# Differential attention normalised from PSUM, and weight chunks split in pieces of 1024 and 512 columns

## The chip, the core and the metric

The kernel runs on one core of a Trainium2 chip. TensorE (PE in the profile) multiplies matrices and writes them to PSUM; VectorE (DVE), ScalarE (ACT) and GpSimd (POOL) work element by element; SyncE (SP) issues most DMAs. GpSimd touches SBUF only. The metric is the device time of one execution in microseconds (us).

## The reference

Two blocks run one after the other on 512 tokens of width 1024, all in float32. The first has a dilated attention layer and a grouped state-space layer. The second has four layers: differential attention, a gated recurrence (hgrn2), a sliding-window attention with sinks, and differential attention again; each is followed by a feed-forward part (1024 to 4096 and back) and a gate. What the change touches most is the differential attention, which occurs twice:

```python
def diff_attention(h, w_in, lam, subln, w_out, rel_bias, layer_idx):
    ...
    lam_full = jnp.exp(jnp.sum(lam32[0] * lam32[1])) - jnp.exp(jnp.sum(lam32[2] * lam32[3])) + lam_init
    for blk in range(S // BLOCK):
        qs = blk * BLOCK
        ke = qs + BLOCK
        s = jnp.einsum('bmqd,bmkd->bmqk', q[:, :, qs:ke], k[:, :, :ke]).astype(jnp.float32)
        ...
        s = jnp.where(rel >= 0, s + bias, -jnp.inf)
        a = jax.nn.softmax(s, axis=-1).reshape(B, H, 2, BLOCK, ke)
        a = a[:, :, 0] - lam_full * a[:, :, 1]
        outs.append(jnp.einsum('bhqk,bhkv->bhqv', a.astype(v.dtype), v[:, :, :ke]))
    ...
```

Eight heads each have two maps of scores (m = 0 and 1). Each is softmaxed by itself, and the second, scaled by lambda, is taken from the first.

## The kernel before, in words

All weights come as one stream of 270 chunks of 128 x 2048 float32 (1 MB). SyncE loads a chunk into one of two raw buffers, raw[0] and raw[1]. GpSimd splits it: the cast (L311) writes the high part wh in the reduced format fp32r, and the subtraction (L313) writes the low part wl = raw - wh. Each large product is then three matmuls (L351 to L353): high by high, low by high, high by low. There are two buffers of wh and wl. GpSimd begins to split chunk c when TensorE has used up chunk c-2 (semaphore w_used); TensorE begins chunk c when w_split says that its subtraction has ended. The very first chunk is split by lines of its own (L318, L323).

The differential attention (function diff_attention) goes in four runs r of two heads each. A run has eight jobs n: head hh = n // 4, block of 128 queries b = n % 4, so a job's scores are w = 128, 256, 384 or 512 columns wide. For a job:

- TensorE computes two maps of scores (L1414) into the PSUM banks 2 + 2 * (n % 2) + m.
- VectorE adds the bias (L1568, L1569) and writes the sum to the SBUF tile SC, then takes the negated row maxima of both maps (L1573).
- ScalarE takes the exponential of both (L1488), in place in SC, with the row sums into sa columns 4 and 5, by an accumulator that a second instruction reads out.
- VectorE normalises in four instructions: the reciprocal of the sums (L1580); times lambda, one column (L1581); the second map times that column (L1582); and the first map times its reciprocal plus the second map (L1583).
- TensorE transposes the result (L1423), ScalarE copies it from PSUM (L1496, tile PT), TensorE multiplies it by V (L1438), and ScalarE copies that out (L1501).

The order on TensorE is written out by hand in pe_jobs: scores(0), scores(1), a piece of the next run's projection; then for each job j: transposes(j), scores(j + 2), a piece of projection (fill), values(j). A run projects for the next run three chunks in eight pieces, the first four of 24 matmuls with 512 columns, the last four of 24 matmuls with 256. In the last run nothing is left to project, and six of the eight finished heads are transposed in its place (turn_head). On VectorE, dve_jobs puts biased(j) behind normalise(j - 1). On ScalarE, act_jobs puts the exponentials of job j ahead of the copy of job j - 1 and the copying out of job j - 2.

Semaphores of a job: SC_FREE after the bias has been added, BIASED after the maxima, EXPED after the exponentials, PNORM after the normalisation, PTC after the copy of the transposes, PV after the product by V. GpSimd has in the differential attention the splits and a few small steps on the heads' norms (L1375, L1376).

Of the kernel before, what the change touches and what calls it, by code (L numbers as in the profile page):

```python
# [14 lines left out]
F32 = mybir.dt.float32  # L15
F32R = mybir.dt.float32r
I32 = mybir.dt.int32
ALU = mybir.AluOpType
ACT = mybir.ActivationFunctionType
# [9 lines left out]
CHUNK = 2048  # L29
# [198 lines left out]
def build(nc, t, out):  # L228

    ctx = ExitStack()  # L230
    with ctx:
# [21 lines left out]
        raw = [sb(f"raw{i}", [P, CHUNK]) for i in range(RAW)]  # L253
        wh = [sb(f"wh{i}", [P, CHUNK], F32R) for i in range(SPLIT)]
# [46 lines left out]
        def load_chunk(sp, c, slot):  # L301

            sp.wait_ge(w_split.h, c - RAW + 1)
            sp.dma_start(raw[slot][:, :], t["weights"][bass.ds(c, 1)].rearrange("a p n -> p (a n)")).then_inc(raw_in[slot].h, 16)

        def split_chunk(pool, c, r, s):

            pool.wait_ge(w_used.h, CREDIT + c - SPLIT + 1)
            pool.wait_ge(raw_in[r].h, 16 * ((c - r) // RAW + 1) if isinstance(c, int) else (c - r) * (16 // RAW) + 16)
            pool.sem_inc(split_ready.h, 1)  # L310
            pool.tensor_copy(wh[s][:, :], raw[r][:, :]).then_inc(w_high.h, 1)  # L311
            pool.wait_ge(w_high.h, c + 1)
            pool.tensor_tensor(wl[s][:, :], raw[r][:, :], wh[s][:, :].bitcast(F32), ALU.subtract).then_inc(w_split.h, 1)  # L313

        def split_high(pool, k):

# [1018 lines left out]
        def diff_attention(layer, j):  # L1335
            c0 = pos[0]
            lam_init = 0.8 - 0.6 * math.exp(-0.3 * layer)
            with ExitStack() as c:
# [20 lines left out]
                with nc.Block() as block:  # L1359
# [26 lines left out]
                    def _(pe):  # L1386
# [19 lines left out]
                        def run(r):  # L1406
                            def wait(s, k):
                                pe.wait_ge(s.h, s.base + RUN * r + k)

                            def scores(n):  # L1410
                                hh, b = n // 4, n % 4
                                wait(SC_FREE, n - 1)
                                for m in range(2):
                                    x = nc.tensor.matmul(PS[2 + 2 * (n % 2) + m][:, 0:P * (b + 1)],  # L1414
                                                         QT[64 * m:64 * m + 64, r % 2, hh, P * b:P * b + P],
                                                         KTT[64 * m:64 * m + 64, r % 2, hh, 0:P * (b + 1)], start=True, stop=True)
                                x.then_inc(SC_DONE.h, 1)

                            def transposes(n):
                                wait(PNORM, n + 1)  # L1420
                                wait(PTC, n)
                                for k in range(n % 4 + 1):
                                    x = nc.tensor.transpose(PS[TBANK][:, P * k:P * k + P], SC[:, n % 2, 0, P * k:P * k + P], ident[:, :])  # L1423
                                x.then_inc(TR.h, 1)

                            def fill(j):
                                for n in range(RUN):
                                    if STEP[n] == j and r + 1 < RUNS:
                                        project(r + 1, n)
                                if r + 1 == RUNS and 0 <= j < 6:  # L1430
                                    turn_head(j)

                            def values(n):
                                wait(PTC, n + 1)
                                wait(OEV, n)
                                hh, b = n // 4, n % 4
                                for k in range(b + 1):
                                    x = nc.tensor.matmul(PS[OBANK][:, 0:P], PT[:, n % 2, P * k:P * k + P],  # L1438
                                                         V[:, r % 2, k, P * hh:P * hh + P], start=(k == 0), stop=(k == b))
                                x.then_inc(PV.h, 1)  # L1440
                            wait(PEV, RUN)
                            pe_jobs(RUN, 2, scores, transposes, values, fill)
# [8 lines left out]
                    def _(act):  # L1451
# [28 lines left out]
                        def run(r):  # L1480
# [3 lines left out]
                            def exps(n):  # L1484
                                wait(BIASED, n + 1)
                                w = P * (n % 4 + 1)
                                for m in range(2):
                                    x = a.activation(SC[:, n % 2, m, 0:w], SC[:, n % 2, m, 0:w], ACT.Exp,  # L1488
                                                     bias=sa[:, n % 2, 2 + m:3 + m], accum_out=sa[:, n % 2, 4 + m:5 + m])
                                x.then_inc(EXPED.h, 1)  # L1490

# [49 lines left out]
                    def _(dve):  # L1541
# [15 lines left out]
                        def run(r):  # L1557
                            def wait(s, k):
                                dve.wait_ge(s.h, s.base + RUN * r + k)

                            def biased(n):
                                hh, b = n // 4, n % 4
                                w = P * (b + 1)
                                wait(SC_DONE, n + 1)
                                wait(TR, n - 1)
                                if n == 0:
                                    dve.wait_ge(BIAS_IN.h, BIAS_IN.base + 16 * (r + 1))
                                link(v.tensor_tensor(SC[:, n % 2, 0, 0:w], PS[2 + 2 * (n % 2)][:, 0:w], B[:, 2 * hh, WD - w:WD], ALU.add))  # L1568
                                v.tensor_tensor(SC[:, n % 2, 1, 0:w], PS[3 + 2 * (n % 2)][:, 0:w], B[:, 2 * hh + 1, WD - w:WD], ALU.add).then_inc(SC_FREE.h, 1)  # L1569
                                wait(SC_FREE, n + 1)  # L1570
                                if n == 7:
                                    dve.sem_inc(BIAS_USED.h, 1)
                                v.tensor_reduce(sa[:, n % 2, 2:4], SC[:, n % 2, :, 0:w], AX.X, ALU.max, negate=True).then_inc(BIASED.h, 1)  # L1573
                                if r + 1 == RUNS and 2 <= n < 8:
                                    low_head(n - 2)

                            def normalise(n):
                                w = P * (n % 4 + 1)
                                wait(EXPED, n + 1)
                                link(v.reciprocal(sa[:, n % 2, 6:8], sa[:, n % 2, 4:6]))  # L1580
                                link(v.tensor_tensor(sa[:, n % 2, 7:8], sa[:, n % 2, 7:8], lam[:, 261:262], ALU.mult))  # L1581
                                link(v.tensor_scalar(SC[:, n % 2, 1, 0:w], SC[:, n % 2, 1, 0:w], sa[:, n % 2, 7:8], None, ALU.mult))  # L1582
                                v.scalar_tensor_tensor(SC[:, n % 2, 0, 0:w], SC[:, n % 2, 0, 0:w], sa[:, n % 2, 6:7],  # L1583
                                                       SC[:, n % 2, 1, 0:w], ALU.mult, ALU.add).then_inc(PNORM.h, 1)
                            dve_jobs(RUN, 2, biased, normalise)
                        for r in range(RUNS):
# [1867 lines left out]
```

## Time and profile before

| | us |
|---|---|
| median of 3 runs | 3903.22 |
| lowest and highest | 3902.64, 3917.36 |
| the profiled execution, own time | 3908.86 |
| its span from first to last instruction | 3907.1 |
| PE busy | 3601.4 |
| DVE busy | 1652.6 |
| ACT busy | 910.5 |
| POOL busy | 1902.8 |

The profile lists the instructions of that one execution. A row of a group gives line, engine, operation, output and input tiles, shapes and count, then the busy time and the mean duration of one. A row of waits says which instruction stood ready behind whose work, how long in all, how many times, and the longest. The granted clock is the share of full speed at which TensorE was let run: 1.0 is 2.4 GHz and 0.5 is 1.2 GHz, and a mean over a stretch lies between. The parts of the program, in us from the start of the span: the dilated attention to 670, the state-space layer to 1040, the first differential attention 1040 to 1290 (its runs 0 to 2 from 1072 to 1237), then feed-forward, hgrn2 from 1760, feed-forward, sliding-window attention from 2570, feed-forward, the second differential attention 3180 to 3440 (its runs 0 to 2 from 3213 to 3385), and the last feed-forward.

### The profile page before, as it was taken

The page shows a single profiled execution, that of the slowest core. Times are in us where ns is not written, and L with a number is a line of the kernel's source. Part 1 is how long each engine was busy: PE and PEld are TensorE (multiplying, and loading weights), DVE is VectorE, ACT ScalarE, POOL GpSimd, SP SyncE. Part 2 cuts the span into 40 slices and gives each one's busy share as a digit, 9 for nine tenths or more (in the row PEclk, how much of TensorE's full clock was granted, in tenths as well). Part 3 has the DMA queues.
Part 4 walks back from the last instruction along what each step waited for, and adds up shares of the span by engine and source line. Part 5 has one row for each costly group of instructions (what it writes and reads, how often), then busy time and mean ns, then how long its engine had stood idle before and what let it go on. Part 6 is the DMA issues. An engine that isn't in the chain of part 4 may idle for free. (4 is left out here: it accounts for less than half of the span.)

```text
span 3907.1 us, 49897 instructions
## 1 busy us (share of the span) xinstructions
PE 3601.4 (92%) x19658; PEld 2934.7 (75%) x19658; DVE 1652.6 (42%) x2665; ACT 910.5 (23%) x2424; POOL 1902.8 (49%) x733
## 2 busy tenths in 40 slices
PE   8899997799998899999957999998999998889999
PEld 6787874677775788878756888776888877678887
DVE  5522326898366411144375211355311326641114
ACT  2333333223134111011251111134101123411101
POOL 5444440523532455555644555532565553245554
PEclk9999995888998999999978999999999999899999
DMA  4236881244221222222202222221222221122222
GB/s 135 92 110 102 109 119 55 68 111 106 104 76 55 90 100 97 97 86 89 86 2 81 87 97 97 87 98 60 87 97 97 97 95 69 55 92 97 97 97 76
DMA packets 96732, 346.76 MB, mean 89 GB/s; under 512 B 27414, under 2 KB 46230, under 8 KB 61720
## 3 DMA queue, kind: packets, MB, share of 16 engines
q1 hardware_dynamic: 84176, 318.31, 27.4%
q10 hardware_dynamic: 12360, 25.70, 1.9%
q8 instruction: 140, 2.29, 0.2%
q14 instruction: 56, 0.46, 0.0%
HBM read 320.90 MB, written 18.87 MB: 87 GB/s over the span
## 5 line engine op out<-in xcount | busy, mean ns | idle before, releaser
L311 POOL CAST wh<-raw 128x2048 fp32r<-128x2048 f32 x269 | 515.7, 1917 | 1623.1 <-PE bank L353 1310.5
L313 POOL TENSOR_TENSOR wl<-raw,wh 128x2048 fp32r<-128x2048 f32 x269 | 1247.1, 4636 | 21.5
L351 PE MATMUL bank<-XTh,wh 128*128 128x512 f32 (+1 forms) x2448 | 951.0, 388 | 32.4 <-DVE XTl L1200 15.1
L352 PE MATMUL bank<-XTh,wl 128*128 128x512 f32 (+1 forms) x2448 | 935.7, 382 | 0.0
L353 PE MATMUL bank<-XTl,wh 128*128 128x512 f32 (+1 forms) x2448 | 935.4, 382 | 0.0
L351 PEld LDWEIGHTS bank<-XTh,wh 128*128 128x128 f32 x2448 | 467.5, 191 | 143.1 <-issue 30.5
L353 PEld LDWEIGHTS bank<-XTl,wh 128*128 128x128 f32 x2448 | 466.4, 191 | 89.8
L352 PEld LDWEIGHTS bank<-XTh,wl 128*128 128x128 f32 x2448 | 467.7, 191 | 84.6
L352 PE MATMUL bank<-wh,HTl 128*128 128x512 f32 x1024 | 403.4, 394 | 0.0
L351 PE MATMUL bank<-wh,HTh 128*128 128x512 f32 x1024 | 401.7, 392 | 0.0
L353 PE MATMUL bank<-wl,HTh 128*128 128x512 f32 x1024 | 397.4, 388 | 0.0
L351 PE MATMUL bank<-wh,XTh 128*128 128x512 f32 (+2 forms) x992 | 367.4, 370 | 29.2 <-DVE XTl L1200 12.6
L353 PE MATMUL bank<-wl,XTh 128*128 128x512 f32 (+2 forms) x992 | 360.7, 364 | 0.0
L352 PE MATMUL bank<-wh,XTl 128*128 128x512 f32 (+2 forms) x992 | 360.6, 364 | 0.0
L1119 ACT ACTIVATE R<-bank 128x512 f32<-128x512 f32 x128 | 76.6, 598 | 946.6 <-PE bank L353 946.6
L1218 DVE TENSOR_TENSOR bank<-R,bank 128x512 f32<-128x512 f32 x128 | 89.1, 696 | 428.8 <-ACT R L1119 428.8
L351 PEld LDWEIGHTS bank<-wh,XTh 128*128 128x128 f32 x992 | 191.7, 193 | 71.2 <-issue 28.1
L351 PEld LDWEIGHTS bank<-wh,HTh 128*128 128x128 f32 x1024 | 192.2, 188 | 44.7
L353 PEld LDWEIGHTS bank<-wl,HTh 128*128 128x128 f32 x1024 | 192.2, 188 | 43.0
L1697 DVE TENSOR_TENSOR SC<-bank,B 128x512 f32<-128x512 f32 (+2 forms) x128 | 59.5, 517 | 382.7 <-PE bank L1653 382.3
L352 PEld LDWEIGHTS bank<-wh,HTl 128*128 128x128 f32 x1024 | 192.5, 188 | 38.1
L353 PEld LDWEIGHTS bank<-wl,XTh 128*128 128x128 f32 x992 | 191.4, 193 | 28.9
(375 smaller groups left out, 4143.0 us busy)
## 6 DMA issues: line engine op xcount, KB each, us to landing
raw<-in_weights SPq DMA_DIRECT2D x270, 1024.0 KB, 4.8
B<-bias_d ACTq DMA_DIRECT2D x8, 1024.0 KB, 5.6
B<-bias_a ACTq DMA_DIRECT2D x8, 512.0 KB, 13.4
bias_d<-O SPq DMA_DIRECT2D x16, 256.0 KB, 21.9
MO<-HS SPq DMA_DIRECT2D x64, 64.0 KB, 2.6
bc<-in_ln_g ACTq DMA_DIRECT2D x8, 512.0 KB, 6.8
bc<-in_ln_b ACTq DMA_DIRECT2D x8, 512.0 KB, 7.7
X<-in_x SPq DMA_DIRECT2D x4, 512.0 KB, 7.9
```

The lines of the kernel that those rows point to most:

```text
L311: pool.tensor_copy(wh[s][:, :], raw[r][:, :]).then_inc(w_high.h, 1)
L313: pool.tensor_tensor(wl[s][:, :], raw[r][:, :], wh[s][:, :].bitcast(F32), ALU.subtract).then_inc(w_split.h, 1)
L351: nc.tensor.matmul(psum, sh, mh, start=first, stop=False)
L352: nc.tensor.matmul(psum, sl, mh, start=False, stop=False)
L353: return nc.tensor.matmul(psum, sh, ml, start=False, stop=last)
L1119: nc.scalar.activation(R[u % 2][:, :], up_bank(q, u)[:, :], ACT.Relu).then_inc(rest["relu"].h, 1)
L1218: v.tensor_tensor(b, R[u % 2][:, :], b, ALU.mult).then_inc(rest["square"].h, 1)
L1697: r = v.tensor_tensor(o, s, b.unsqueeze(1).to_broadcast([P, m, w]), ALU.add)
```

## The change

It has two edits. The first lets ScalarE write the exponentials to the two PSUM banks that held the job's scores, instead of to SC. VectorE then reads them there: the product by 1/sum and the product by lambda are one instruction with two scalar columns, which writes SC, and the last instruction takes its first map from PSUM. The scores of job n, which overwrite the banks of job n - 2, wait for the normalisation (PNORM) of job n - 2 where they waited for its SC_FREE. The second edit divides each chunk's cast into two instructions of 1024 columns and its subtraction into four of 512. The semaphores are raised by the last piece, so nobody downstream gets a part of a chunk earlier.

```diff
+        def pieces(n):
+            return [slice(CHUNK // n * i, CHUNK // n * (i + 1)) for i in range(n)]
+
         def split_chunk(pool, c, r, s):
...
             pool.sem_inc(split_ready.h, 1)
-            pool.tensor_copy(wh[s][:, :], raw[r][:, :]).then_inc(w_high.h, 1)
+            for half in pieces(2):
+                x = pool.tensor_copy(wh[s][:, half], raw[r][:, half])
+            x.then_inc(w_high.h, 1)
             pool.wait_ge(w_high.h, c + 1)
-            pool.tensor_tensor(wl[s][:, :], raw[r][:, :], wh[s][:, :].bitcast(F32), ALU.subtract).then_inc(w_split.h, 1)
+            for quarter in pieces(4):
+                x = pool.tensor_tensor(wl[s][:, quarter], raw[r][:, quarter], wh[s][:, quarter].bitcast(F32), ALU.subtract)
+            x.then_inc(w_split.h, 1)
...
                             def scores(n):
                                 hh, b = n // 4, n % 4
-                                wait(SC_FREE, n - 1)
+                                wait(PNORM, n - 1)
...
                                 for m in range(2):
-                                    x = a.activation(SC[:, n % 2, m, 0:w], SC[:, n % 2, m, 0:w], ACT.Exp,
+                                    x = a.activation(PS[2 + 2 * (n % 2) + m][:, 0:w], SC[:, n % 2, m, 0:w], ACT.Exp,
                                                      bias=sa[:, n % 2, 2 + m:3 + m], accum_out=sa[:, n % 2, 4 + m:5 + m])
...
                                 link(v.reciprocal(sa[:, n % 2, 6:8], sa[:, n % 2, 4:6]))
-                                link(v.tensor_tensor(sa[:, n % 2, 7:8], sa[:, n % 2, 7:8], lam[:, 261:262], ALU.mult))
-                                link(v.tensor_scalar(SC[:, n % 2, 1, 0:w], SC[:, n % 2, 1, 0:w], sa[:, n % 2, 7:8], None, ALU.mult))
-                                v.scalar_tensor_tensor(SC[:, n % 2, 0, 0:w], SC[:, n % 2, 0, 0:w], sa[:, n % 2, 6:7],
+                                link(v.tensor_scalar(SC[:, n % 2, 1, 0:w], PS[3 + 2 * (n % 2)][:, 0:w], sa[:, n % 2, 7:8], lam[:, 261:262],
+                                                     ALU.mult, ALU.mult))
+                                v.scalar_tensor_tensor(SC[:, n % 2, 0, 0:w], PS[2 + 2 * (n % 2)][:, 0:w], sa[:, n % 2, 6:7],
                                                        SC[:, n % 2, 1, 0:w], ALU.mult, ALU.add).then_inc(PNORM.h, 1)
```

## Rows read from the trace of the kernel before

**Rows 1.** The page's first part: busy us (share of span) x instructions of each engine

```profile
PE 3601.4 (92%) x19658; PEld 2934.7 (75%) x19658; DVE 1652.6 (42%) x2665; ACT 910.5 (23%) x2424; POOL 1902.8 (49%) x733
```

**Rows 2.** Waits of PE, 1072 to 1237, then 3213 to 3380: us, times, longest

```profile
PE bank L1423 <- DVE SC L1583: 10.4, 9, 4.2
PE bank L1438 <- ACT PT L1496: 4.4, 5, 1.2
...
PE bank L1423 <- DVE SC L1583: 15.9, 8, 5.7
```

**Rows 3.** Timeline from 1181.9 (start, us, instruction, [idle before])

```profile
1181.94 2.01 DVE L1582 TENSOR_SCALAR SC<-SC,sa 128x128 f32<-128x128 f32 x1
...
1183.94 4.50 POOL L313 TENSOR_TENSOR wl<-raw,wh 128x2048 fp32r<-128x2048 f32 x1
1183.98 4.61 DVE L1583 SCALAR_TENSOR_TENSOR SC<-SC,sa 128x128 f32<-128x128 f32 x1
...
1188.65 0.47 PE L1423 MATMUL bank<-ident,SC 128*128 128x128 f32 x1 [4.22 <-DVE SC L1583]
```

**Rows 4.** Single lines of the attention: duration ns min/median/max, first and last start, forms

```profile
L1582 DVE TENSOR_SCALAR SC<-SC,sa x64: 286/420/4807, 1079.2 to 3422.5; 128x128 f32<-128x128 f32 x16, 128x256 f32<-128x256 f32 x16, 128x384 f32<-128x384 f32 x16, 128x512 f32<-128x512 f32 x16
...
L1583 DVE SCALAR_TENSOR_TENSOR SC<-SC,sa x64: 350/617/4612, 1079.5 to 3423.1; 128x128 f32<-128x128 f32 x16, 128x256 f32<-128x256 f32 x16, 128x384 f32<-128x384 f32 x16, 128x512 f32<-128x512 f32 x16
...
L1581 DVE TENSOR_TENSOR sa<-sa,lam x64: 158/159/3554, 1075.6 to 3422.3; 128x1 f32<-128x1 f32 x64
```

**Rows 5.** Single lines outside it, the same columns

```profile
L1218 DVE TENSOR_TENSOR bank<-R,bank x128: 695/696/697, 1354.7 to 3796.8; 128x512 f32<-128x512 f32 x128
...
L1189 DVE SCALAR_TENSOR_TENSOR bank<-bank,st,bc x64: 747/759/760, 1322.8 to 3850.5; 128x512 f32<-128x512 f32 x64
```

**Rows 6.** Groups by shape, DVE, 1239 to 1277 (last run, no chunk): busy us, mean ns

```profile
L1583 DVE SCALAR_TENSOR_TENSOR SC<-SC,sa 128x512 f32<-128x512 f32 x2 | 1.5, 750 | 0.1
...
L1582 DVE TENSOR_SCALAR SC<-SC,sa 128x512 f32<-128x512 f32 x2 | 1.0, 486 | 0.1
```

**Rows 7.** Stretches: us, busy us (instructions) of each engine, granted clock, DMA share, GB/s

```profile
1190.00:1200.00 10.00, 10.00 (x37) 6.89 (x33) 3.24 (x8) 2.67 (x9) 1.25 (x1) 0.74 0.24 96
...
1072.00:1237.00 165.00, 149.52 (x850) 119.74 (x849) 108.32 (x168) 59.17 (x214) 61.75 (x20) 0.97 0.22 75
3213.00:3385.00 172.00, 152.02 (x848) 122.21 (x848) 113.91 (x168) 59.16 (x214) 61.23 (x20) 0.94 0.21 70
...
670.00:1040.00 370.00, 327.21 (x1993) 267.68 (x1994) 290.92 (x373) 92.11 (x180) 156.24 (x74) 0.89 0.37 105
```

**Rows 8.** The sigmoid on ScalarE: duration ns min/median/max

```profile
L1126 ACT ACTIVATE Y<-bank x16: 598/598/604, 1710.5 to 3869.2; 128x512 f32<-128x512 f32 x16
L1126 ACT ACTIVATE bank<-bank x16: 582/582/582, 1744.2 to 3902.0; 128x512 f32<-128x512 f32 x16
```

**Rows 9.** GpSimd: a one-column instruction, a chunk under the feed-forward, who waited for L313

```profile
L958 POOL TENSOR_SCALAR st<-st x32: 191/192/193, 1322.9 to 3850.2; 128x1 f32<-128x1 f32 x32
...
1506.57 1.90 POOL L311 CAST wh<-raw 128x2048 fp32r<-128x2048 f32 x1 [4.45 <-PE bank L353]
1508.55 4.63 POOL L313 TENSOR_TENSOR wl<-raw,wh 128x2048 fp32r<-128x2048 f32 x1
...
  PE bank L351: 5.3, 5
```

**Rows 10.** Timelines of the norm at 728, the sinks, the first attention

```profile
728.09 4.33 DVE L831 SCALAR_TENSOR_TENSOR N<-X,st,bc 128x1024 f32<-128x1024 f32 x1
...
732.48 1.97 PE L754 MATMUL bank<-ident,N 128*128 128x128 f32 x8 [3.49 <-DVE N L831]
...
2597.95 4.07 DVE L1709 TENSOR_SCALAR stats<-stats,sk 128x2 f32<-128x2 f32 x1
...
117.73 4.81 DVE L1721 TENSOR_TENSOR SC<-SC,stats 128x512 f32<-128x512 f32 x1
```

**Rows 11.** Timeline of DVE in the state-space layer

```profile
752.42 4.87 DVE L2859 TENSOR_TENSOR W<-scratch 128x512 f32<-128x512 f32 x1
```

## The prediction

> **What bounds the kernel now.** The page's first part comes first: TensorE is busy 92% of the span, VectorE 42%, GpSimd 49% [rows 1]. The So time comes back only where TensorE stands still, or runs at half clock after standing still. PE was not busy for 306 us in all (3907.1 less 3601.4), and the change touches one place directly: the two differential attentions, some 250 us each. Each has four runs of eight jobs. In runs 0 to 2 TensorE also projects the next run's queries, keys and values, and GpSimd splits their weight chunks beside it; the fourth run has no projection and no chunk.
>
> The waits of PE in runs 0 to 2 name one releaser above all: the transposes (L1423) waited 10.4 and 15.9 us for VectorE's last step of the normalisation (L1583) [rows 2]. The timeline tells why. At 1181.94 the normalisation's second product (L1582, 128x128) took 2.01 us, and its third (L1583) took 4.61 us; GpSimd's subtraction had started at 1183.94 and took 4.50. PE stood still for 4.22 us [rows 3]. The quickest L1582 took 286 ns and the quickest L1583 350 ns, and their longest 4807 and 4612, about one subtraction more [rows 4]. Lines with one input in PSUM never stretch: in the feed-forward, where GpSimd is busy six tenths of the time (6.5 of 11 us a chunk [rows 9]), L1218 (one input in each memory) took 695 to 697 ns in all 128 executions [rows 5]. So a VectorE instruction is held by GpSimd here when it has two inputs in SBUF (L1581, L1583), or is the product L1582 from SBUF to SBUF with one tensor and one scalar column, which runs at 490 ns for 512 columns, faster than one column per cycle of L1583's 750 [rows 6]. It is held for the rest of the GpSimd instruction.
>
> **Edit 1: normalisation from PSUM.** It removes L1581 and gives both remaining products one input in PSUM. By the rows above none is then held. The new wait of the scores costs nothing: scores(n) now wait for normalise(n-2), and transposes(n-2), which stand ahead of them in PE's queue, wait for the same count; at a run's start the count was passed in the run before.
> - Removed PE waits: 10.4 + 15.9 = 26.3 us in 17 waits [rows 2]. Two or three of 0.2 us belong to no hold, so I take **25**. The waits of L1438 on ScalarE's copy (4.4 us in the first stage) stay.
> - Clock. After the 4.22 us pause the granted clock was 0.74 of full in 1190 to 1200 [rows 3, 7]. Over runs 0 to 2 it averaged 0.97 and 0.94 [rows 7]: 165 x 0.03 + 172 x 0.06 = 15.3 us of full-clock time not granted. Part of it fell in the pauses themselves or follows other waits; I take **12**, between 6 and 15.
> - Own durations. L1581 goes: 159 ns and about 35 ns between two instructions. L1582 from PSUM has no row here. Its lower end is its time now, 286 ns for 128 columns and 486 for 512; the upper end is L1583's, 350 and 750 [rows 4, 6]. I take the upper end, since L1583 is the same work at one column per cycle: +64 to +264 ns, 164 on average over the four widths, less 194. That is -0.03 us a job. Only the two last runs, with no projection beside the chain, have VectorE's own time on the path, 16 jobs: **0**, between -3 and +2. The Trainium skill, "VectorE: DVE Perf Modes", section on the perf-mode tier table, says a PSUM operand takes tensor_scalar with fp32 out of its double rate; no row here shows it, and it agrees with the end that I took. By the other end, 16 jobs would be 2.6 us shorter.
> - ScalarE writes the exponentials to PSUM. The nearest rows are its sigmoid: 582 ns to PSUM, 598 to SBUF [rows 8]. Two per job, at most 0.03 us: nothing, and a hidden gain in runs 0 to 2.
>
> **Edit 2: pieces.** It acts on 269 chunks, all but the very first. The cast (1.90 us) becomes two, the subtraction (4.61 us) four. Four more instructions cost, at the 0.19 us that a one-column instruction takes there [rows 9], at most 0.8 us a chunk. A part of that may overlap with the piece before, down to nothing; I take 0.5. (The Trainium skill, "GPSIMD Engine Reference", section 3.1, gives 4497 ns for a two-input instruction of 2048 columns and some 2.6 cycles per element, which at its 1.2 GHz leaves only 0.06 us of fixed cost; by that, 0.2 us a chunk, and the sum is 1.3 us lower.)
> - Under the feed-forward, GpSimd waits 4.45 us for PE, casts for 1.90 and subtracts for 4.63, so a chunk comes every 11 us [rows 9]: 0.5 us more is hidden, and up to 4 us would be.
> - PE waited for the split at 5 places, 5.3 us in all [rows 9]. Each grows by 0.5: **+2.5**, between 0 and 4.
> - Holds outside the differential attentions. Where one product alone is urgent, it now waits for a quarter (some 1.2 us) instead of 4.6. The cases with a PE wait behind: the first block's norm at 728, L831 4.33 us, PE waiting 3.49; the sink attention at 2598, L1709 4.07 us for two columns; the first attention at 117.7 and once more at 191.9, L1721 4.8 us for 512 columns [rows 10]. If each is held 1.2 us at most, the savings are about 2, 3, 2 and 2 us; half-clock stretches behind them may go too: **-9**, between 0 and -15.
> - Where VectorE's queue is dense, in the state-space block (670 to 1040, VectorE busy 291 of 370 us), pieces give little. One instruction pays for a whole subtraction today (L2859 4.87 us) [rows 11]. With pieces, each of the next ones with two SBUF inputs can meet a quarter: the same 4.6 us in four parts. And each piece of GpSimd can wait for VectorE in turn. **0**, between -8 and +8.
>
> **Sum.** -25 - 12 + 0 + 2.5 - 9 + 0 = -43.5. The profiled execution took 3908.86 us (span 3907.1); it becomes 3865. It stands 5.6 us above the median of the three runs shown, 3903.2, which becomes 3860.
>
> **Rivals.**
> - A, the next engine takes the place. After a hold, ScalarE's exponentials and copy, or the late projection steps of half length, are next: jobs 3 to 6 of a run have only 2.6 us of projection beside them. Half of the 37 us of edit 1 returns as waits of L1438 on ScalarE. Against it: the jobs without a hold ran beside the same projections with waits of 0.2 to 1.2 us only. 3903 - 18 - 6.5 = 3878.
> - B, the pieces bring nothing elsewhere, since each urgent product meets the next piece as well. 3903 - 37 + 2.5 = 3869.
> - C, the change doesn't do what it says: a product that reads PSUM but takes its two scalar columns from SBUF and writes SBUF is held as before, and only the pieces shorten the hold, from 4.4 to some 1.2 us. For it speaks that no row shows L1582's form from PSUM; against it L1189 (PSUM, a scalar column and one SBUF tensor), never over 760 ns in 64 executions [rows 5]. About 60% of the 37 us: 3903 - 22 - 6.5 = 3875.
> - D, slower. VectorE and GpSimd alternate in the state-space block, and a chunk of six pieces waits up to six times for one of VectorE's instructions of 0.75 us (L1583's time for 512 columns [rows 6]): 6.5 us becomes 7 + 4.5 = 11.5. PE needs a chunk each 11 us where it is fed fully; from there it starves. At most 24 chunks are split there (156 us at 6.5); an excess of 2.8 us each is 67 us, more than the 43 gained: 3927. Against it: PE itself waits for VectorE there, and GpSimd was busy 156 of 370 us, so it has room to double nearly [rows 7].
>
> **Chances.** The forecast 0.62, A 0.13, B 0.15, C 0.06, D 0.04. Half a per cent, about what a measurement of this kernel can tell from no change, is 19.5 us: the bound is 3883.7. The forecast, B and most of A and C lie below: faster 0.87. Within: the upper tails of A and C and a small D, 0.10. Slower 0.03. Range: the low end has all of the clock (15), all the waits (26), 15 elsewhere and 8 in the state-space block: 3903 - 26 - 15 - 15 - 8 + 2 = 3841. The high end takes in A and C with the bad ends of the small terms: 3887.
>
> **What would show it.** In the profile after, both products of the normalisation keep to narrow durations (351 to some 750 ns). The waits of the transposes on VectorE in runs 0 to 2 fall to 1 or 2 us in all, and the clock there rises towards 0.99. The cast is at some 1.0 us and the subtraction at 1.2 us apiece, a chunk at 7 us. VectorE's longest holds elsewhere fall from 4.3 to some 1.2 us, but there are more of them. The forecast is wrong if ScalarE's waits grow in the attention, if a product there still takes over 1 us, or if the weight loads wait for the split in more than a handful of places.

## The result, and the profile after

The changed kernel takes **3860.8 us** (median of 4 runs, 3857.1 to 3865.5); the kernel before, beside it, 3902.9 (4 runs). The ratio is 0.9889, with a 95% interval of 0.9864 to 0.9913. The forecast was 3860. A right total does not show that its terms were right: four of them were off by 7 to 8 us each, and the misses cancel (the last part has the sum). The profiled execution of the changed kernel (after, below) took 3865.5 us (span 3863.4). In the code of after, the lines from the attention on stand 7 further down: L1583 is L1590, L1423 is L1430, L351 is L358, L3223 is L3230. The two GpSimd lines L311 and L313 are L315 and L319.

VectorE is busy 127 us less, though it does nearly the same work, and GpSimd 183 us more (the page's first part, after; against [rows 1]):

```profile
PE 3597.6 (93%) x19658; PEld 2933.2 (76%) x19658; DVE 1525.5 (39%) x2601; ACT 909.0 (24%) x2424; POOL 2086.0 (54%) x1809
```

The two normalisation lines of after, and one line of the feed-forward that read PSUM before already: duration in ns, minimum/median/maximum.

```profile
L1588 DVE TENSOR_SCALAR SC<-bank,sa,lam x64: 409/611/811, 1065.5 to 3375.9; 128x128 f32<-128x128 f32 x16, 128x256 f32<-128x256 f32 x16, 128x384 f32<-128x384 f32 x16, 128x512 f32<-128x512 f32 x16
...
L1590 DVE SCALAR_TENSOR_TENSOR SC<-bank,sa,SC x64: 349/551/752, 1066.0 to 3376.8; 128x128 f32<-128x128 f32 x16, 128x256 f32<-128x256 f32 x16, 128x384 f32<-128x384 f32 x16, 128x512 f32<-128x512 f32 x16
...
L1225 DVE TENSOR_TENSOR bank<-R,bank x128: 695/696/697, 1327.3 to 3752.7; 128x512 f32<-128x512 f32 x128
```

No maximum is near the 4807 and 4612 of [rows 4]. Runs 0 to 2 of both attentions, cut at the same matmuls as in [rows 7] (us, busy us and instructions of PE, PEld, DVE, ACT, POOL, granted clock, DMA share, GB/s), and PE's waits in the first of the stretches:

```profile
1062.00:1208.00 146.00, 142.39 (x849) 115.60 (x848) 73.11 (x144) 58.19 (x214) 66.46 (x56) 1.00 0.24 85
3193.00:3339.00 146.00, 142.39 (x848) 115.78 (x849) 73.14 (x144) 58.20 (x214) 66.49 (x56) 1.00 0.25 85
```

```profile
PE bank L1445 <- ACT PT L1503: 2.1, 3, 0.7
PE bank L1430 <- DVE SC L1590: 1.1, 3, 0.4
```

The pair took 337 us (165 + 172) and takes 292: 45 less. In [rows 7] PE was busy 301.5 us of it and stood still 35.5; now it is busy 284.8 and stands still 7.2. So 28 us were standing time, and 17 us were matmuls that had run at half clock: the clock is 1.00 in both stretches, where it was 0.97 and 0.94.

Outside of these runs the two profiled executions are nearly level (they are 44 us apart in all), but only in sum. Cut at the same matmuls, in us against before (the second profile is of the same changed kernel):

| stretch of before | after | both edits, second profile | edit 1 alone | edit 2 alone |
|---|---|---|---|---|
| start to 670 (first attention) | +0.1 | -3.3 | -2.5 | -3.4 |
| norms, 670 to 736 | -2.8 | -3.1 | -0.3 | -2.5 |
| state-space block, 736 to 1040 | -7.3 | -8.0 | +1.1 | -12.9 |
| differential attention, runs 0 to 2, both | -44.9 | -44.9 | -44.9 | -29.6 |
| its last runs, both | +0.6 | +0.8 | +1.8 | -0.2 |
| four feed-forwards | +10.1 | +9.1 | +0.1 | +8.9 |
| sink attention, 2570 to 2704 | +1.7 | +1.2 | 0.0 | +1.2 |

### The profile page after: what moved, and what is told of

Its sections match the earlier page's. It is cut to its first block and busy times, and to the rows that moved or that the text cites. A ratio compares the mean times of both kernels' runs of the same rounds, so it can differ in the third digit from the quotient of the medians.

```text
span 3863.4 us, 50909 instructions
## 1 busy us (share of the span) xinstructions
PE 3597.6 (93%) x19658; PEld 2933.2 (76%) x19658; DVE 1525.5 (39%) x2601; ACT 909.0 (24%) x2424; POOL 2086.0 (54%) x1809
## 5 line engine op out<-in xcount | busy, mean ns | idle before, releaser
L319 POOL TENSOR_TENSOR wl<-raw,wh 128x512 fp32r<-128x512 f32 x1076 | 1388.9, 1322 | 21.8
L315 POOL CAST wh<-raw 128x1024 fp32r<-128x1024 f32 x538 | 558.2, 1067 | 1418.1 <-PE bank L360 1106.1
L358 PE MATMUL bank<-XTh,wh 128*128 128x512 f32 (+1 forms) x2448 | 951.0, 388 | 39.7 <-DVE XTl L1207 15.1
L358 PEld LDWEIGHTS bank<-XTh,wh 128*128 128x128 f32 x2448 | 468.8, 191 | 149.1 <-issue 26.5
L358 PE MATMUL bank<-wh,HTh 128*128 128x512 f32 x1024 | 401.7, 392 | 0.0
L358 PE MATMUL bank<-wh,XTh 128*128 128x512 f32 (+2 forms) x992 | 365.3, 368 | 28.2 <-DVE XTl L1207 12.6
L358 PEld LDWEIGHTS bank<-wh,XTh 128*128 128x128 f32 x992 | 189.4, 191 | 70.5 <-issue 28.1
L358 PEld LDWEIGHTS bank<-wh,HTh 128*128 128x128 f32 x1024 | 192.2, 188 | 44.7
```

Of the source, the lines that this page charges most:

```text
L315: x = pool.tensor_copy(wh[s][:, half], raw[r][:, half])
L319: x = pool.tensor_tensor(wl[s][:, quarter], raw[r][:, quarter], wh[s][:, quarter].bitcast(F32), ALU.subtract)
L358: nc.tensor.matmul(psum, sh, mh, start=first, stop=False)
```

## The experiments

They ran in three groups on three chips, each beside the kernel before, whose medians there were 3905.3, 3907.4 and 3903.9 us. Across chips it is the ratios that compare. "Runs 0 to 2" means these runs of both differential attentions, always cut at the same matmuls.

### Each edit alone

Edit 1 alone keeps the whole chunks:

```diff
-            for half in pieces(2):
-                x = pool.tensor_copy(wh[s][:, half], raw[r][:, half])
-            x.then_inc(w_high.h, 1)
+            pool.tensor_copy(wh[s][:, :], raw[r][:, :]).then_inc(w_high.h, 1)
...
```

> The changed kernel with each chunk split whole again (one cast, one subtraction): edit 1 alone. Theory (edit 1 brings all of the gain of the two differential attentions, 45 us in runs 0 to 2 by the stretches of the two traces; the pieces win some 10 us in the state-space layer and its norms and lose some 10 in the feed-forwards and at the start): 3858 to 3862 us, the same as the changed kernel within 5 us. Its runs 0 to 2 last 146 us each set, and the waits of the weights on the split in the feed-forwards are back at 1.14 us. Rival (the pieces carry a good part of it): 3875 us or more.

Measured: 3865.8 us (3862.2 to 3872.4), ratio 0.9903 (0.9886 to 0.9920). The median is 4 us above what I expected; runs 0 to 2 gain what they should. Edit 2 alone, the pieces with the old normalisation:

> The kernel before with the chunks split in pieces: edit 2 alone. Theory: outside the differential attentions the pieces bring nothing in sum, inside them a held product waits for a quarter (1.3 us) and not for a whole subtraction, but two or three products of a job can each be held: about half of the 45 us comes back, 3875 to 3885 us. Rival (the hold is shared out, each of the three lines meets the next piece, so the sum of the holds stays): 3895 to 3905 us. Rival (a quarter is short enough to hide entirely behind the other work): 3862 us, as good as edit 1.

Measured: 3874.5 us (3868.9 to 3881.5), ratio 0.9927 (0.9910 to 0.9944). The product that took up to 4807 ns takes up to 1546 (the line below). The gains do not add up: 39.5 and 30.8 us apart, 42 to 44 together, because both take the same waits of runs 0 to 2 (44.9 and 29.6 in the table). After edit 1, the pieces find nothing there. Outside, edit 2 gains in the state-space block and loses in the feed-forwards.

```profile
L1589 DVE TENSOR_SCALAR SC<-SC,sa x64: 285/454/1546, 1056.5 to 3380.1; 128x128 f32<-128x128 f32 x16, 128x256 f32<-128x256 f32 x16, 128x384 f32<-128x384 f32 x16, 128x512 f32<-128x512 f32 x16
```

### Is it GpSimd's subtraction that holds them?

The normalisation stays as before, and the suspected cause shrinks:

```diff
-            pool.tensor_tensor(wl[s][:, :], raw[r][:, :], wh[s][:, :].bitcast(F32), ALU.subtract).then_inc(w_split.h, 1)
+            pool.tensor_tensor(wl[s][:, 0:low], raw[r][:, 0:low], wh[s][:, 0:low].bitcast(F32), ALU.subtract).then_inc(w_split.h, 1)
```

with `low` = 64 in the differential attentions and 2048 elsewhere. What this kernel leaves out is the low part of all other columns of the attentions' weights.

> The kernel before, its normalisation untouched. What is left out: in the two differential attentions GpSimd subtracts only the first 64 of a chunk's 2048 columns (the cast is whole), so the low parts of those weights are not made. If the runs' waits for the normalisation come from GpSimd's subtraction holding the vector instructions (my theory), runs 0 to 2 of both attentions together gain about 45 us (as both edits and edit 1 alone measured) with nothing changed in the normalisation, their two main instructions never take over 1 us, and the whole lands near 3860. If the gain of edit 1 came from shorter or earlier normalisation by itself, or from ScalarE's writing to PSUM (rival), less than 15 us are gained here and the time stays at 3890 or more.

Measured: 3867.0 us in one run, 7 above what I expected; one run bears no interval, so the reading rests on the stretches. Runs 0 to 2 gain 45.5 us, as much as with edit 1, with the old normalisation in SBUF. Its two lines:

```profile
L1582 DVE TENSOR_SCALAR SC<-SC,sa x64: 285/421/1991, 1074.9 to 3377.9; 128x128 f32<-128x128 f32 x16, 128x256 f32<-128x256 f32 x16, 128x384 f32<-128x384 f32 x16, 128x512 f32<-128x512 f32 x16
```

```profile
L1583 DVE SCALAR_TENSOR_TENSOR SC<-SC,sa x64: 350/552/753, 1075.3 to 3378.4; 128x128 f32<-128x128 f32 x16, 128x256 f32<-128x256 f32 x16, 128x384 f32<-128x384 f32 x16, 128x512 f32<-128x512 f32 x16
```

The product still reaches 1991 ns: the cast, 1.9 us long and still whole, holds it too (my "never over 1 us" was wrong), but PE's waits for the normalisation come to only 0.7 us in runs 0 to 2 of the first attention. Six products of job 4 still start 0.03 us from a subtraction, as before; it is now so short that they lose 0.15 us. So the cause is shown: what edit 1 gains in these runs, the subtraction had cost.

### Which operand counts, and when

Two halves of edit 1, each with whole chunks. In the first, the last instruction reads two SBUF inputs and the product reads PSUM; in the second, the product works from SBUF to SBUF and the last instruction reads PSUM.

```diff
-                                    x = a.activation(PS[2 + 2 * (n % 2) + m][:, 0:w], SC[:, n % 2, m, 0:w], ACT.Exp,
+                                    x = a.activation(PS[3 + 2 * (n % 2)][:, 0:w] if m else SC[:, n % 2, 0, 0:w], SC[:, n % 2, m, 0:w], ACT.Exp,
...
-                                v.scalar_tensor_tensor(SC[:, n % 2, 0, 0:w], PS[2 + 2 * (n % 2)][:, 0:w], sa[:, n % 2, 6:7],
+                                v.scalar_tensor_tensor(SC[:, n % 2, 0, 0:w], SC[:, n % 2, 0, 0:w], sa[:, n % 2, 6:7],
```

> Edit 1 alone, but the first map's exponentials are written to SBUF again, so that the last instruction of the normalisation has two inputs in SBUF, while the product of the second map reads PSUM. Theory (two SBUF inputs are enough to be held for the rest of GpSimd's instruction): that last instruction shows maxima near 5 us, the product keeps below 0.85 us, and most of the gain is lost, 3890 to 3905 us. Rival (it was only the product from SBUF to SBUF that was held, and the others stood in its queue): 3858 to 3862 us and no long durations.

Measured: 3868.1 us (3863.7 to 3875.5).

```diff
-                                    x = a.activation(PS[2 + 2 * (n % 2) + m][:, 0:w], SC[:, n % 2, m, 0:w], ACT.Exp,
+                                    x = a.activation(SC[:, n % 2, 1, 0:w] if m else PS[2 + 2 * (n % 2)][:, 0:w], SC[:, n % 2, m, 0:w], ACT.Exp,
...
-                                link(v.tensor_scalar(SC[:, n % 2, 1, 0:w], PS[3 + 2 * (n % 2)][:, 0:w], sa[:, n % 2, 7:8], lam[:, 261:262],
+                                link(v.tensor_scalar(SC[:, n % 2, 1, 0:w], SC[:, n % 2, 1, 0:w], sa[:, n % 2, 7:8], lam[:, 261:262],
```

> Edit 1 alone, but the second map's exponentials are written to SBUF again: the product, with one tensor input, reads SBUF and writes SBUF, and the last instruction has one input in PSUM. Theory (a product from SBUF to SBUF in its fast form, 490 ns for 512 columns, is held as well): the product shows maxima near 5 us, the last instruction keeps below 0.76 us, time 3890 to 3905 us. Rival (only two SBUF inputs are held): no duration of the product over 0.85 us, 3856 to 3862 us.

Measured: 3857.0 us (3854.6 to 3862.6). Single lines of the first, then of the second:

```profile
L1584 DVE TENSOR_SCALAR SC<-bank,sa,lam x64: 409/610/812, 1081.2 to 3387.8; 128x128 f32<-128x128 f32 x16, 128x256 f32<-128x256 f32 x16, 128x384 f32<-128x384 f32 x16, 128x512 f32<-128x512 f32 x16
...
L1586 DVE SCALAR_TENSOR_TENSOR SC<-SC,sa x64: 350/619/4500, 1081.7 to 3388.7; 128x128 f32<-128x128 f32 x16, 128x256 f32<-128x256 f32 x16, 128x384 f32<-128x384 f32 x16, 128x512 f32<-128x512 f32 x16
```

```profile
L1584 DVE TENSOR_SCALAR SC<-SC,sa,lam x64: 345/482/3627, 1069.5 to 3367.6; 128x128 f32<-128x128 f32 x16, 128x256 f32<-128x256 f32 x16, 128x384 f32<-128x384 f32 x16, 128x512 f32<-128x512 f32 x16
...
L1586 DVE SCALAR_TENSOR_TENSOR SC<-bank,sa,SC x64: 350/551/752, 1073.1 to 3368.2; 128x128 f32<-128x128 f32 x16, 128x256 f32<-128x256 f32 x16, 128x384 f32<-128x384 f32 x16, 128x512 f32<-128x512 f32 x16
```

The operand rule of the prediction holds line by line: what reads PSUM keeps to 752 or 812 ns, and the two forms that work from SBUF can both be held, up to 4500 and 3627. But I had expected each half to give back most of the gain, and neither did: runs 0 to 2 gain 39.6 and 46.3 us. The reasons differ.

In the first half the last instruction is held as often as was feared: in 12 of its 64 executions by more than 1 us, 36 us in all. PE hardly pays for it. Its waits for the normalisation in runs 0 to 2 of the first attention, against 10.4 us in nine waits before [rows 2]:

```profile
PE bank L1426 <- DVE SC L1586: 2.7, 3, 2.0
```

Each of these runs has one hold of 3.8 to 3.9 us, in job 2, and there PE goes on with other work: it does not stand still ahead of that job's transposes. Before, each run has a second one, in job 4, and PE stands still for 1.6 to 1.9 us ahead of its transposes. A hold costs what the slack of its job does not cover.

In the second half the product is seldom held, six times by more than 1 us. The rival that this left is the moment at which the instruction meets GpSimd. The timelines show it (start, us, instruction). Before, job 4 of run 1 of the first attention:

```profile
1153.56 1.89 POOL L311 CAST wh<-raw 128x2048 fp32r<-128x2048 f32 x1 [7.76 <-PE bank L353]
...
1154.99 0.47 DVE L1581 TENSOR_TENSOR sa<-sa,lam 128x1 f32<-128x1 f32 x1
...
1155.50 4.69 DVE L1582 TENSOR_SCALAR SC<-SC,sa 128x128 f32<-128x128 f32 x1
1155.53 4.58 POOL L313 TENSOR_TENSOR wl<-raw,wh 128x2048 fp32r<-128x2048 f32 x1
```

The same job with the product in SBUF and lambda inside it:

```profile
1142.84 1.89 POOL L314 CAST wh<-raw 128x2048 fp32r<-128x2048 f32 x1 [7.22 <-PE bank L356]
1144.07 0.17 DVE L1583 RECIPROCAL sa<-sa 128x2 f32<-128x2 f32 x1 [3.73 <-ACT SC L1491]
1144.28 0.54 DVE L1584 TENSOR_SCALAR SC<-SC,sa,lam 128x128 f32<-128x128 f32 x1
1144.81 4.58 POOL L316 TENSOR_TENSOR wl<-raw,wh 128x2048 fp32r<-128x2048 f32 x1
```

Before, the one-column product with lambda (L1581, 0.16 us when free) has two SBUF inputs and is held to the end of the cast, at 1155.45. So the product L1582 starts within 0.03 us of the subtraction and waits for all of it. Without L1581, the product is itself the one that waits out the cast's tail (0.54 instead of 0.35 us), and what follows it reads PSUM. Seven of the 13 holds of over 4 us that L1582 has before are of this kind (six in job 4, one in job 7). The other six are in job 2. There L1581 isn't held; its own 0.2 us are enough to put the product behind the start of the subtraction. Before, then without L1581:

```profile
1141.03 0.16 DVE L1581 TENSOR_TENSOR sa<-sa,lam 128x1 f32<-128x1 f32 x1
1141.20 4.61 POOL L313 TENSOR_TENSOR wl<-raw,wh 128x2048 fp32r<-128x2048 f32 x1
1141.22 4.80 DVE L1582 TENSOR_SCALAR SC<-SC,sa 128x384 f32<-128x384 f32 x1
```

```profile
1130.66 0.48 DVE L1584 TENSOR_SCALAR SC<-SC,sa,lam 128x384 f32<-128x384 f32 x1
1130.82 4.79 POOL L316 TENSOR_TENSOR wl<-raw,wh 128x2048 fp32r<-128x2048 f32 x1
```

With 0.16 us of a start the product runs free. One more kernel tests this: it puts lambda's instruction back. The product then has one scalar column again in place of two, which is no rival, since both forms are held somewhere (4807 and 3627 ns).

```diff
-                                link(v.tensor_scalar(SC[:, n % 2, 1, 0:w], SC[:, n % 2, 1, 0:w], sa[:, n % 2, 7:8], lam[:, 261:262],
-                                                     ALU.mult, ALU.mult))
+                                link(v.tensor_tensor(sa[:, n % 2, 7:8], sa[:, n % 2, 7:8], lam[:, 261:262], ALU.mult))
+                                link(v.tensor_scalar(SC[:, n % 2, 1, 0:w], SC[:, n % 2, 1, 0:w], sa[:, n % 2, 7:8], None, ALU.mult))
```

> The kernel with the product in SBUF, the last instruction from PSUM, whole chunks everywhere (3857 with the factor lambda inside the product), but with lambda multiplied in by an instruction of its own ahead of the product, as in the kernel before. If it is the 0.2 us that this puts the product later that sets it beside the start of GpSimd's subtraction (my theory), the product is again held 4.4 us in about half of the maps, the six runs give back 15 to 40 of their 46 us, and the time is 3872 to 3895. If the product could run free because only one of its operands is read from SBUF (rival), the fold does not matter: it is held at most twice, as with the factor inside, and the time stays at 3855 to 3862.

Measured: **3898.6 us** (3893.9 to 3909.8), ratio 0.9987 (0.9975 to 0.9999) against 0.9883 with lambda inside: some 41 us more, and 4 us above the slow end of what I expected. Runs 0 to 2 keep 13.8 of the 46 us; the other 32 are most of the difference. The product has its 13 long holds again, in the same jobs. Its timeline:

```profile
1151.89 1.89 POOL L314 CAST wh<-raw 128x2048 fp32r<-128x2048 f32 x1 [7.76 <-PE bank L356]
...
1153.32 0.47 DVE L1584 TENSOR_TENSOR sa<-sa,lam 128x1 f32<-128x1 f32 x1
...
1153.83 4.69 DVE L1585 TENSOR_SCALAR SC<-SC,sa 128x128 f32<-128x128 f32 x1
1153.86 4.58 POOL L316 TENSOR_TENSOR wl<-raw,wh 128x2048 fp32r<-128x2048 f32 x1
```

It is the old pattern to 0.01 us. An instruction on one column, 0.16 us long, decides over 32 us in these runs. (The Trainium skill, "SBUF — State Buffer", section "Who interferes with whom", says that a VectorE instruction with two SBUF inputs, or a tensor_scalar in a two-port mode, contends with GpSimd's reads, and that whoever issues first has the shared ports for the whole instruction. The rows agree: 4.69 us beside a subtraction of 4.58. The recorded starts do not tell who issued first: L1582 is recorded 0.03 us ahead of L313 and was the one that waited.)

### Where the pieces gain and where they cost

Edit 1 whole, the pieces in the state-space stage alone (eight chunks, split between 736 and 890 us):

```diff
-        def split_chunk(pool, c, r, s):
+        def split_chunk(pool, c, r, s, casts=1, subs=1):
...
-            for half in pieces(2):
+            for half in pieces(casts):
...
-            for quarter in pieces(4):
+            for quarter in pieces(subs):
...
-                stream(pool, c0 + AHEAD, c0 + AHEAD + N, 2, lambda k, j: split_chunk(pool, k, j % RAW, j % SPLIT))
+                stream(pool, c0 + AHEAD, c0 + AHEAD + N, 2, lambda k, j: split_chunk(pool, k, j % RAW, j % SPLIT, 2, 4))
```

> The exponentials and products as in the changed kernel; pieces of 1024 and 512 columns only in the state-space stage, whole chunks in all others. If the pieces gain only in the state-space stage (7 to 13 us there in the changed kernel and with edit 2 alone) and cost in the feed-forwards (1.7 to 3 us each, about 10 together), this has both: 3850 to 3858, at least 4 us below the changed kernel run beside it. If the state-space stage's gain comes from pieces elsewhere or is chance, it equals edit 1 alone, 3862 to 3868, and the stage takes what it takes before.

> As the run before it, but the second map's exponentials and product stay in SBUF and only the last instruction reads PSUM. By the gains measured so far (3857 with whole chunks, and 7 to 10 us of the state-space stage by pieces): 3846 to 3853, the fastest of all. If the short hold of the product that whole chunks allowed was luck of the timing, it is not better than the run before it: 3850 to 3860.

> The changed kernel itself, beside the others on the same chip: 3858 to 3864. Against edit 1 alone (3865.8, on another chip) it tells whether the pieces bring anything beyond edit 1: by the sum of the stages (minus 8 in the state-space stage, plus 10 in the feed-forwards, some us either way elsewhere) it should be within 5 us of it.

Measured, on one chip: pieces in the state-space stage alone 3856.9 us (3855.6 to 3858.5); the same with the product in SBUF 3852.1 (3846.8 to 3861.5); the changed kernel again 3863.4 (3859.4 to 3866.1). The block takes 12.9, 10.3 and 8.0 us less than before; the four feed-forwards stand at +1.7, -0.1 and +9.1. So keeping the chunks whole outside is worth 6.5 us, and the two ranges do not meet. Whether both edits beat edit 1 alone cannot be told: 0.9889 and 0.9896 against 0.9903, with intervals that overlap.

The profiles agree on the block. In all seven with the subtraction cut it is 7.3 to 12.9 us shorter than before; in the six others besides before itself (five with whole chunks, one with only the cast cut) it is between 2.9 shorter and 1.1 longer. What falls are PE's waits for VectorE's products of the weights (L3063 <- L3223, in after L3070 <- L3230): us, times, longest, over 736 to 1045, before, then with pieces everywhere. The 18.1 is the longest of the six profiles with whole chunks (10.5 to 18.1); the five with pieces of 1024 and 512 have 4.5 to 6.7.

```profile
PE bank L3063 <- DVEq L3223: 18.1, 3, 7.7
```

```profile
PE bank L3070 <- DVEq L3230: 6.6, 2, 3.4
```

GpSimd's groups in the block (shape, count, busy us, mean ns, idle before) say who pays for it. Before, then after:

```profile
L313 POOL TENSOR_TENSOR wl<-raw,wh 128x2048 fp32r<-128x2048 f32 x16 | 77.0, 4812 | 1.3
L311 POOL CAST wh<-raw 128x2048 fp32r<-128x2048 f32 x15 | 30.9, 2060 | 170.1 <-PE bank L353 122.9 <-DMA raw<-in_weights 47.2
```

```profile
L319 POOL TENSOR_TENSOR wl<-raw,wh 128x512 fp32r<-128x512 f32 x64 | 99.6, 1585 | 1.3
L315 POOL CAST wh<-raw 128x1024 fp32r<-128x1024 f32 x30 | 36.3, 1237 | 135.2 <-PE bank L360 94.8 <-DMA raw<-in_weights 40.4
```

The same 16 chunks take GpSimd 28 us more, of which 16 x 0.73 = 12 us are the pieces' own cost; its idle time of 170 us falls to 135. VectorE's busy time in the block falls from 238.5 to 227.8 us. VectorE gets its turn between two pieces, and the delay goes to the engine that had time.

Three more kernels, all with the product in SBUF, vary the pieces in this stage: only the subtraction cut (`1, 4`), only the cast (`2, 1`), and smaller pieces (`4, 8`).

> The kernel with the product in SBUF and the last instruction from PSUM; in the state-space stage only the subtraction is cut (four pieces of 512 columns), the cast is whole; whole chunks elsewhere. If the length of the subtraction is what keeps VectorE's work for L3070's transposes waiting (its whole form takes 4.6 us, the cast 1.9), the stage gains nearly all it gained with both cut (10.3 us): 8 to 11, and the time is 3850 to 3855. If the cast's halves bring it, 0 to 3 us and 3857.

> The same with only the cast cut (two pieces of 1024) in the state-space stage, the subtraction whole. By the theory that the subtraction's length decides: a gain of 0 to 3 us in the stage, its three waits of L3070's transposes stay near 7, 6 and 4 us as before the change, time 3855 to 3860. By the rival (each more boundary between GpSimd's instructions lets VectorE in, whichever instruction is cut) a third of the gain, 3 to 4 us.

> The same with the cast in four pieces of 512 and the subtraction in eight of 256 columns in the state-space stage. Each piece more costs about 0.18 us, so a chunk takes about 7.24 + 2 x 0.18 + 4 x 0.18 = 8.3 us. If the waits left with 2 and 4 pieces (2.3 us each) are still holds, they shrink below 2 and the stage gains 1 to 3 us more, time 3849 to 3852. If GpSimd's longer chunk now comes late (rival), waits for the split appear in the stage and the gain falls by 2 to 10 us: 3854 to 3862.

| pieces of cast, subtraction | time (range), us | ratio | block, us against before | PE's waits for L3230, us |
|---|---|---|---|---|
| 1, 1 | 3857.0 (3854.6 to 3862.6) | 0.9883 | -2.9 | 10.5 |
| 2, 1 | 3858.4 (3856.7 to 3860.6) | 0.9879 | -2.9 | 8.5 |
| 1, 4 | 3853.4 (3851.3 to 3859.3) | 0.9870 | -9.6 | 8.4 |
| 2, 4 | 3852.1 (3846.8 to 3861.5) | 0.9867 | -10.3 | 4.5 |
| 4, 8 | **3847.6** (3847.4 to 3850.5) | 0.9851 | -10.3 | 1.4 |

In the block the subtraction's length decides, as expected: 9.6 us against the 2.9 that whole chunks have too. In the whole times the two kernels' intervals overlap. The waits alone would not have said so either: they are equal in rows two and three, and the rest of the difference is the clock, 0.87 in the block with only the cast cut and 0.90 with only the subtraction cut. (With whole chunks it lies between 0.87 and 0.89, so part of this may be chance.) With 4 and 8 pieces the waits all but vanish, yet the block gains no more, where I had expected 1 to 3 us: PE's waits for the hidden state's transfer (L3102) take 4.6 us there. That run has the lowest median, 13 to 16 us below the changed kernel's two, with an interval of 0.9834 to 0.9867. Its 4 us below `2, 4` can't be told: the intervals overlap, and the two ran on two chips. The rival did not come: the chunk grew well beyond the 8.3 us of my estimate, since GpSimd is now the one that waits (the four pieces of the cast and the eight of the subtraction, in one row each):

```profile
749.66 4.12 POOL L315 CAST wh<-raw 128x512 fp32r<-128x512 f32 x4 [0.89 <-PE bank L360]
753.87 7.70 POOL L319 TENSOR_TENSOR wl<-raw,wh 128x256 fp32r<-128x256 f32 x8
```

That is 11.9 us for a chunk that takes 6.7 in one piece beside the same work, and PE still never waited for it in this block.

## Why the prediction was right, point by point

- **Waits and clock of runs 0 to 2** (-25 and -12). Mechanism right, and shown from two sides: the PSUM operands free the products, and so does the short subtraction. Both sizes were low. Standing time fell by 28 us, since the waits for ScalarE's copy that I kept (4.4 us in the first attention) fell too, to 2.1. With the short subtraction and the old normalisation they are 2.1 as well, so they came from the held jobs. The half clock gave 17 us where I had taken 12: I had discounted part of it as fallen "in the pauses themselves", but of the 32 us at half clock in these runs only 3 fell while PE stood still, and all 32 are gone. 45 instead of 37.
- **Own durations** (0). The product from PSUM takes 409 to 811 ns, 60 above my upper end (350 to 750). That end came from an instruction with one scalar column; this one has two. The last runs cost 0.6 to 1.8 us more, inside the -3 to +2.
- **Later chunks** (+2.5, at most 4). Wrong by 8 us: the four feed-forwards cost 10.1. The working counted the waits for the split, and in the feed-forwards these did what it said: 1.14 us became 1.68, and in the first 1.98 (5.3 us in all became 10.3, but 2.2 of that growth is at the start of the program, where the time of the first transfer varies). With one new wait of 0.4 that is 2.8 us for the four. What it left out is the clock: a half-clock stretch of 3.4 us, 1.7 us each, stands behind a pause of 2.1 us (or behind the wait for the split) in 7 of the 12 feed-forwards of the three profiles with pieces everywhere, and in 3 of the 44 of the eleven with whole chunks there. In after it stands in three; two of them (columns as above):

```profile
1306.00:1312.00 6.00, 5.14 (x30) 5.17 (x31) 5.10 (x9) 0.00 (x0) 5.92 (x6) 0.72 0.01 4
2108.00:2114.00 6.00, 5.17 (x31) 5.20 (x32) 5.07 (x9) 0.00 (x0) 5.92 (x6) 0.72 0.00 0
```

  That is 5.1 of the 10.1 us. Why the clock falls there more often with pieces, no run here settles, nor the last 2 us. A chunk itself costs what I took, a little more: 2 x 1041 + 4 x 1291 = 7246 ns against some 6510, so 0.18 us for each further instruction, near the 0.19 of [rows 9]. (The Trainium skill, "GPSIMD Engine Reference", section 3.1, has 4497 ns for 2048 columns and some 2.6 cycles per element, from which my estimate was 0.06; the trace does not bear the estimate out.)

```profile
L319 POOL TENSOR_TENSOR wl<-raw,wh x1076: 1257/1291/2261, 26.2 to 3842.5; 128x512 fp32r<-128x512 f32 x180
...
  PEld bank L358: 20.8, 9
  PE bank L358: 10.3, 6
```

```profile
L315 POOL CAST wh<-raw x538: 1033/1041/2057, 24.1 to 3837.7; 128x1024 fp32r<-128x1024 f32 x180
```

- **Holds elsewhere** (-9, 0 to -15). The norms gave 2.8 us. The sink attention cost 1.7 where I had counted 3 of gain. The first attention differs from run to run by more than its term (from 3.0 us less to 5.7 more than before among the ten kernels whose chunks are whole there, and that change nothing there), so the 4 us put on it cannot be told. All stages outside of the six runs, the block and the feed-forwards gave 1.6 us together.
- **State-space block** (0). The step that failed is "the same 4.6 us in four parts". It is true of VectorE's sum only if its next instructions are as many and as urgent; PE waited at three places where one instruction was held by a whole subtraction (L2859 for 4.87 us [rows 11], L2856 twice for 4.87 and 4.88), and there a quarter is all that stands in front. It brought 7.3 us in the profiled run, and 8.0 and 12.9 in the two other profiles with pieces everywhere: at and beyond my bound of 8.
- **Rivals.** C fell: 409 to 811 ns, and whole chunks with edit 1 alone give the full 44.9 us. A fell: ScalarE's waits became shorter. D fell: a chunk does take up to 10.6 us in the block in after (11.9 with the smaller pieces), but GpSimd has the room. Its 67 us had no working either: 11.5 against the 11 that PE needs is an excess of 0.5 us a chunk, not 2.8, some 12 us in 24 chunks. B was half right: on top of edit 1 the pieces bring nothing that the intervals can tell, since the gain in the block and the norms (10 us) meets the loss in the feed-forwards (10 us).

So the mechanism of edit 1 was right, and the total came out by luck, because the misses cancel: 8 us more gain in the attention and 7 in the block, against 8 more loss in the feed-forwards and 7 less gain elsewhere.

## What to carry to other kernels

Ask of each urgent VectorE instruction whether it takes two inputs, or a fast copy-like form, from SBUF while GpSimd is at work; one PSUM operand frees it for the price of a slower form (the product takes 409 to 811 ns instead of 286 to 486). Then ask what a hold costs there: one that falls in a job with work to spare for TensorE cost nearly nothing here. Where operands can't move, cut the GpSimd instruction, but only in the stages where someone urgent meets it: elsewhere each piece costs 0.18 us, and a late chunk can cost a stretch at half clock. And look at what runs just before the held instruction: one that waits out the tail of one GpSimd instruction sets its successor beside the head of the next, and folding it away can be worth the whole gain.

## What the runs showed of the hardware

- An instruction of one column with two SBUF inputs is held like a long one (0.47 instead of 0.16 us beside a cast), and one that starts within 0.03 us of a GpSimd instruction can wait for all of it, even if its recorded start is the earlier one.
- No instruction of the normalisation was held for longer than one GpSimd instruction, so pieces bound the hold of the product: 4807 ns with 4.6 us subtractions, 1546 with quarters, 1991 with a short subtraction and a whole cast. The next VectorE instruction can be held again by the next one of GpSimd: with edit 2 alone the three instructions of a job lose 0.5, 1.1 and 0.9 us in turn.
- GpSimd pays in turn: in the state-space block, beside dense VectorE work, its quarters take 1585 ns on average; their median over the whole program is 1291.
- The product with two scalar columns from PSUM costs 60 ns more than scalar_tensor_tensor with one (409 against 349 ns for 128 columns, 811 against 752 for 512).
